# Two expert slabs of the second pair held outside the ring, loaded from GpSimd's queue

## What is computed

```python
logits = (xt @ w_router + b_router)             # 256 tokens, 32 experts
top_val, top_idx = lax.top_k(logits, 4)
gates = jax.nn.softmax(top_val, axis=-1)
...
def expert_block(args):
    xb, e = args
    hcat = xb @ w_in[e] + b_in[e]               # w_in[e]: 1024 x 2048
    x_glu = jnp.minimum(hcat[:, :D_FF], SWIGLU_LIMIT)
    x_lin = jnp.clip(hcat[:, D_FF:], -SWIGLU_LIMIT, SWIGLU_LIMIT)
    act = x_glu * jax.nn.sigmoid(SWIGLU_ALPHA * x_glu) * (x_lin + 1)
    return act @ w_out[e] + b_out[e]            # w_out[e]: 1024 x 1024
```

## Time and profile before

| | us |
|---|---|
| median of the 3 runs | 2167.94 |
| lowest and highest run | 2167.68, 2172.42 |
| profiled execution, device time | 2166.01 |
| span of its trace, first to last instruction | 2164.2 |

### The profile page before, as it was taken

How to read it: one execution, slowest core, us unless ns; L and a number is a source line. 1 busy time by engine, 2 the same in 40 slices (tenths; PEclk the granted TensorE clock), 3 DMA queues, 4 the chain that set the end, 5 groups by cost and what they waited for, 6 DMA issues and landing times.

```text
span 2164.2 us, 24146 instructions
## 1 busy us (share of the span) xinstructions
PE 2000.6 (92%) x9756; PEld 1265.9 (58%) x9756; DVE 628.3 (29%) x1299; ACT 405.4 (19%) x763; POOL 174.4 (8%) x225
## 2 busy tenths in 40 slices
PE   6999998888889898888888999999999999989998
PEld 4645643333334333333333467588788888868887
DVE  3767432111222122211122254522104316310321
ACT  3125211101111111110111120221113214320210
POOL 0000000000000000000000000000563941000000
PEclk9999999999999999999999999999999999989999
DMA  9985679999999999999999994942344342634320
GB/s 364 345 313 212 277 310 414 417 419 419 419 415 417 417 418 417 417 417 419 419 419 417 415 386 143 355 164 100 123 148 156 134 158 79 233 117 154 109 107 20
DMA packets 164389, 627.80 MB, mean 290 GB/s; under 512 B 5248, under 2 KB 9472, under 8 KB 127840
## 3 DMA queue, kind: packets, MB, share of 16 engines
q1 hardware_dynamic: 163856, 625.39, 73.8%
q0 software_dynamic: 464, 1.44, 0.2%
HBM read 625.76 MB, written 1.05 MB: 290 GB/s over the span
## 4 chain that ended last, share of the span: by engine, by line
PE 71%; DMA 16%; DVE 7%; issue 3%; ACT 2%; SPq 1%; DVEq 0%; ACTq 0%
PE psum L1007 31%; PE psum L1332 22%; DMA ring<-in_w_in_dram 14%; PE psum L1018 3%; PE psum L1309 2%; PE psum L1445 1%; PE psum L1220 1%; PE psum L1107 1%; DVE arena L2369 1%; PE psum L1620 1%; PE psum L1046 1%; DMA ring<-in_w_qkv_dram 1%; DVE arena L2384 1%; SPq L874 1%; DMA sq<-in_w_in_dram 1%
## 5 line engine op out<-in xcount | busy, mean ns | idle before, releaser
L1332 PE MATMUL psum<-ring,arena 128*64 128x512 f32 x3136 | 707.3, 608 | 90.7 <-DMA ring<-in_w_in_dram 89.9
L1007 PE MATMUL psum<-arena,ring 128*128 128x256 f32 (+1 forms) x3072 | 684.3, 385 | 6.5 <-ACT arena L1699 4.8
L1007 PEld LDWEIGHTS psum<-arena,ring 128*128 128x128 f32 x3072 | 585.3, 191 | 103.6 <-issue 22.5
L1332 PEld LDWEIGHTS psum<-ring,arena 128*64 128x64 f32 x3136 | 238.5, 140 | 546.5 <-issue 509.4
L1822 ACT ACTIVATE arena<-psum 128x512 f32<-128x512 f32 (+1 forms) x155 | 88.5, 571 | 835.8 <-PE psum L1332 726.5
L2369 DVE TENSOR_TENSOR arena<-psum,arena 128x512 f32<-128x512 f32 (+1 forms) x68 | 42.8, 668 | 431.5 <-PE psum L1354 421.7
L2356 DVE TENSOR_SCALAR arena<-consts,arena 128x64 f32<-128x64 f32 (+1 forms) x68 | 16.7, 309 | 335.0 <-PE psum L1332 335.0
L2642 DVE SCALAR_TENSOR_TENSOR consts<-psum,smalls,consts 128x255 f32<-128x255 f32 (+1 forms) x88 | 38.4, 478 | 232.7 <-ACT consts L1966 231.9
L2802 POOL DMA_DIRECT2D arena<-in_pos_dram x1 | 0.6, 577 | 1022.5 <-PE psum L1424 1022.5
L1309 PE MATMUL psum<-arena 128*128 128x256 f32 (+1 forms) x288 | 70.4, 387 | 12.0 <-DVE arena L2345 10.7
L1739 ACT ACTIVATE arena<-psum 128x512 f32<-128x512 f32 (+1 forms) x57 | 31.8, 562 | 231.6 <-PE psum L1007 175.8
(11 more groups left out here) (369 smaller groups left out, 1582.5 us busy)
## 6 DMA issues: line engine op xcount, KB each, us to landing
ring<-in_w_in_dram SPq DMA_DIRECT2D x130, 2048.0 KB, 16.2
ring<-in_w_out_dram SPq DMA_DIRECT2D x66, 2048.0 KB, 17.9
ring<-in_w_ada_dram SPq DMA_DIRECT2D x36, 2048.0 KB, 13.7
ring<-in_w_up_dram SPq DMA_DIRECT2D x22, 2048.0 KB, 8.1
ring<-in_w_ret_dram SPq DMA_DIRECT2D x12, 2048.0 KB, 15.0
ring<-in_w_down_dram SPq DMA_DIRECT2D x16, 1408.0 KB, 6.0
ring<-in_w_qkv_dram SPq DMA_DIRECT2D x4, 2048.0 KB, 19.9
ring<-in_w_rout_dram SPq DMA_DIRECT2D x4, 2048.0 KB, 9.4
```

The costliest lines, as they stand in the source:

```text
L1007: ins = nc.tensor.matmul(bank(c)[:, at:at + n], w[:, k, m * P:m * P + P], r, start=(k == 0), stop=(k == k_tiles - 1))
L1332: ins = nc.tensor.matmul(psum[at:at + CAP, p, :], act[:, k, CAP * e:CAP * e + CAP], w[:, n0:n0 + BANK], start=(k < 3 - halves), stop=(k >= ...
```

## The change

- `EARLY_SLABS` is 1: slab 2 of pair 0 still goes into the arena; slab 3 of pair 0 now goes through the ring. `slot_at` turns by one so that the slots of the later parts stay where they were.
- Two slabs of pair 1 are held outside the ring (`HELD_EXPERT = (3, 7)`, both of expert 3): slab 3 in `h_moe` and `sq` (two transfers of 1 MiB), slab 7 in `con("decay")`, `b_out_sb` and the end of `rstd` (transfers of 1 MiB, 0.5 MiB and 0.5 MiB). GpSimd issues them: slab 3 when (`htok`, 3) is ready, slab 7 when `x_ready` is 8.
- SP writes out pair 1, leaves these two out, and begins its loop at pair 2. Slab 9 of pair 1 goes into the slot that slab 3 leaves free and waits for `rows_done` 4 only. In pair 0, behind `up(0)` (`rows_done` 1) come slabs 7 and 8, behind `up(1)` slab 9, behind `up(2)` slabs 10 and 11; before, slabs 8 and 9 came behind `up(0)` and slabs 10 and 11 behind `up(2)`.
- TensorE writes out pair 1 too, with its own waits and tiles (`second_full`, `second_tile`).
- The list of extra jobs moves on DVE from behind pair 0 to behind its loop, since its buffers now hold slabs of pair 1.
- `decay` is loaded after ("rv", 0) of the retention part.

```diff
-EARLY_SLABS = 2
+EARLY_SLABS = 1
 MOE_SLABS = 12 * PAIRS - EARLY_SLABS
+HELD_EXPERT = (3, 7)
...
-    return (n + 2) % RING
+    return (n + 1) % RING
...
+        held_expert_w = [[(0, 0, flat(h_moe)), (1, 0, flat(sq))],
+                         [(0, 0, con("decay")), (1, 0, b_out_sb), (1, 1024, flat(rstd))]]
...
-                if n == 17:
-                    sp.dma_start(consts[:, at_decay:], const[:, at_decay:]).then_inc(decay_in, 16)
...
-                if q == RING:
-                    read_ready(sp, ("htok", 3))
-                    for kk, out in enumerate(early_w[1]):
-                        sp.dma_start(out, expert_source(1, 1)[:, kk, :]).then_inc(early_in[1], 16)
...
-                    sp.wait_ge(moe.rows_done, 1 if q < 8 else 3)
+                    sp.wait_ge(moe.rows_done, {6: 1, 7: 1, 8: 2, 9: 3, 10: 3}[q])
                 load(SLABS_1 + q, expert_source(j % 2, j // 2))
...
+            for j in range(12):
+                if j in HELD_EXPERT:
+                    continue
+                if j - 6 in HELD_EXPERT:
+                    sp.wait_ge(moe.rows_done, 4)
+                else:
+                    pair_left(1, j)
+                load(MOE_0 + j, expert_source(2 + j % 2, j // 2))
+            with sp.Fori(2, PAIRS) as i:
...
+                if key == ("rv", 0):
+                    sp.dma_start(consts[:, at_decay:], const[:, at_decay:]).then_inc(decay_in, 16)
...
+            experts(moe, 2, 1, second_full, second_tile)
+            with pe.Fori(2, PAIRS) as i:
...
             experts(moe, 2, 0, (0, 1), 0, (2, 3), 0, first=True)
+            with dve.Fori(1, PAIRS - 1) as i:
+                experts(moe, 2, i, (i * 2, i * 2 + 1), 0, (i * 2 + 2, i * 2 + 3), 0)
             own.mark(V.memset(sums_of[:, :, 0:64], 1.0))
...
+            for n, j in enumerate(HELD_EXPERT):
+                if n == 0:
+                    read_ready(pool, ("htok", 3))
+                else:
+                    pool.wait_ge(moe.x_ready, 8)
+                w = w_in[2 + j % 2].rearrange("(k p) n -> p k n", p=P)
+                for kk, at, out in held_expert_w[n]:
+                    pool.dma_start(out, w[:, UP_TILES * (j // 2) + kk, at:at + out.shape[1]]).then_inc(held_in[n], 16)
```

More of the change, by code:

```diff
@@ L342, in places @@
             slot[SLAB_KEYS[n]], full[SLAB_KEYS[n]] = slot_at(n), 16 * loads[slot_at(n)]
+    for j in HELD_EXPERT:
+        loads[slot_at(MOE_0 + j)] -= 1
     queue = [(slot_at(MOE_0 + n), None) for n in range(RING)]
@@ L628, in transformer_blocks_kernel @@
         over_ready = sem("over_ready")
-        early_in = [sem(f"early_in{n}") for n in range(2)]
+        early_in = sem("early_in")
+        held_in = [sem(f"held_expert_in{n}") for n in range(len(HELD_EXPERT))]
         pos_ready = sem("pos_ready")
@@ L1396, in first_full, with first_tile, loads_of, second_full @@
                     pe.wait_ge(ring_full[slot_at(n)], 16 * (n // RING + 1))
-            def first_tile(j, k_tiles, kk):
+            def first_tile(j, k_tiles, kk, n0):
                 if j == 2:
-                    return early_w[0][:, kk, :]
-                if j == 3:
-                    return early_w[1][kk]
-                return in_rows(slot_at(SLABS_1 + j if j < 2 else MOE_0 + j), k_tiles)[:, kk, :]
+                    return early_w[:, kk, n0:n0 + BANK]
+                return in_rows(slot_at(SLABS_1 + j if j < 2 else MOE_0 + j), k_tiles)[:, kk, n0:n0 + BANK]
+            def loads_of(j, held):
+                n = MOE_0 + j
+                return n // RING + 1 - sum(h % RING == j % RING for h in held)
+            def second_full(j):
+                if j in HELD_EXPERT:
+                    n = HELD_EXPERT.index(j)
+                    pe.wait_ge(held_in[n], 16 * len(held_expert_w[n]))
+                else:
+                    held = [h for h in HELD_EXPERT if h < j]
+                    pe.wait_ge(ring_full[slot_at(MOE_0 + j)], 32 + 16 * loads_of(j, held))
+            def second_tile(j, k_tiles, kk, n0):
+                if j not in HELD_EXPERT:
+                    return tile_in_ring(j, k_tiles, kk, n0)
+                for tile_k, at, w in held_expert_w[HELD_EXPERT.index(j)]:
+                    if tile_k == kk and at <= n0 < at + w.shape[1]:
+                        return w[:, n0 - at:n0 - at + BANK]
             copied(pe, ("cols", 5))
             experts(moe, 2, 0, first_full, first_tile, first=True)
-            with pe.Fori(1, PAIRS) as i:
+            experts(moe, 2, 1, second_full, second_tile)
+            with pe.Fori(2, PAIRS) as i:
                 def full(j):
-                    n = MOE_0 + j
-                    pe.wait_ge(ring_full[slot_at(n)], i * 32 + 16 * (n // RING + 1))
+                    pe.wait_ge(ring_full[slot_at(MOE_0 + j)], i * 32 + 16 * loads_of(j, HELD_EXPERT))
                 experts(moe, 2, i, full, tile_in_ring)
@@ L2438, in _ @@
             V.tensor_copy(jobs, jobs_f).then_inc(over_ready, 1)
-            with dve.Fori(1, PAIRS - 1) as i:
-                experts(moe, 2, i, (i * 2, i * 2 + 1), 0, (i * 2 + 2, i * 2 + 3), 0)
             dve.wait_ge(over_ready, 1)
```

37 lines of the change are left out of this document (18 added, 19 removed).

## The result

| | before | changed | difference |
|---|---|---|---|
| median, us | 2168.55 (2167.68 to 2172.42, 6 runs) | 2158.56 (2154.97 to 2161.78, 6 runs) | -9.99 |
| ratio to before | | 0.995 [0.9941, 0.996] | |
| profiled execution: time, span, us | 2166.01, 2164.2 | 2154.97, 2153.2 | span -11.0 |

The forecast was 2167.9 - 8.3 = 2159.6 us, with 2155.5 to 2165 as its range. It is faster by 0.5%, beyond the 0.3% that the prediction took as what a measurement can tell. The six runs of the changed kernel lie in two groups, three at 2155.0 to 2156.2 us and three at 2160.9 to 2161.8; the median stands between them.

What follows compares the result with a forecast made beforehand. Expert weight transfers at 418 GB/s were taken to bound the kernel until 1200 us. Three idle holes of 14.4 us would shrink to 6.1, gaining 8.3: 2167.9 - 8.3 = 2159.6 us, range 2155.5 to 2165.

Steps and rivals of the forecast that it cites:

- Step 1: Up to 280 us: transfers unchanged in sum, up(1)'s wait for the transfer into sq gone, TensorE 0.7 us earlier.
- Step 2: First idle hole, 280 to 284 us: slabs 7 and 8 of pair 0 still wait for up(0), so 3.3 us stay.
- Step 3: Second idle hole, 292 to 299 us: its 4.6 us vanish, as slab 9 of pair 0 waits for up(1) only.
- Step 4: Third idle hole, 318 to 326 us, 6.5 us: held slab 7 fills it, leaving holes of 0.5 and 1.9 us.
- Step 5: Turn into pair 2: TensorE no longer waits in pair 1; a 0.4 us hole remains at pair 2's slab 2.
- Step 6: Held slabs' transfers from GpSimd: the ring's rate and a start of some 4 us, hidden under work already queued.
- Steps 7 and 8: DVE's moved list (6.0 us, up to 6.0 without cover) and decay's later load (2.5 us of the engines): both cost nothing.
- Step 9: GpSimd's waits and TensorE's written-out pair 1: cost nothing, bound 1 us.
- Rival B: Held slab 7 starts too late for the third hole: gain 5.6, 2162.3 us; or clock falls in pair 1's turn, 2161.3; chance 0.27.
- C: GpSimd's queue moves the held slab slowly, up(3) of pair 1 waits, engines run dry at 365.9: slower, 2210 us; chance 0.05.
- D: The holes did not set the steady stretch's start, TensorE was late instead: nothing moves, 2167.9 us; chance 0.05.

Runs made afterwards that it cites:

- held_always: The changed kernel with slabs 3 and 7 held outside the ring in every pair from 1 to 13, issued by GpSimd: 2159.86 us, ratio 0.9949 to before.
- the extra slabs: The changed kernel with eight more unread 2 MiB slabs, one in each of pairs 4 to 11: 2196.38 us issued by GpSimd, 2198.70 us by SP.
- changed_third: The changed kernel run again with no edit, its third comparison: 2157.99 us against 2168.55 before, ratio 0.9957.
- moves_only: The kernel before with only DVE's list behind its loop and decay loaded later, no slab held: 2169.16 us against 2168.68, ratio 1.0.

## Why the prediction was right, point by point

- **What bounds** (transfers until 1200 us, everything behind shifted with them): right. In the comparisons and the traces the lack of 240 to 400 us and the time go together: 14.2 us of lack before and 14.2 with the moves alone (no gain), 2.7 and 4.2 in the changed kernel (10 to 11.5 us), 9.2 with one slab (4.7 us). "Everything behind shifted" holds for the work, but not to the microsecond: from the last `up(3)` to the end the traces differ by up to 4.8 us, mostly with the clock.
- **Step 1** (no wait for `sq`): right, the wait is gone.
- **Step 2** (the first hole of 3.3 us stays): this term was mis-sized. It measured 276 to 284 at 401 GB/s in after, at 333 and 345 in the two repeats: 0.3 to 1.6 us. The 3.3 of before held the fall of the clock at the first gather (0.72), which I took as given; with that clock in `held_always` 2.7 us stayed.
- **Step 3** (second hole gone, since slab 9 waits for `up(1)` only): right; undoing it opened 3.4 us there.
- **Step 4** (third hole closed but for 0.5 and 1.9): right for the hole, too high for what remains. Slabs 4 and 5 were issued at 325.12 in after, 327.86 and 328.08 in the repeats (predicted 329.1); in after they found the stream still busy. 326 to 330 lacks 4 x (1 - 350/418) = 0.7 us in after, 1.3 and 1.4 us in the repeats (281 and 274 GB/s).
- **Step 5** (0.4 at pair 2's slab 2): 370 to 376 moves 370 GB/s in after, a lack of 0.7 us, and 389 and 393 in the repeats, 0.4 us: right.
- **The sum**: 6.1 us of holes were to stay, 2.7 to 4.2 did, by what steps 2 and 4 had too high; small lacks that the ledger does not have (340 to 360 us at 400 to 408 GB/s) took part of it back. Where the chain of waits is read instead, the forecast is closer than its terms: pair 2's `up(3)` was to start at 409 and the last wait to end at 1192; it was 405.1, 407.9 and 408.2, and 1188.2, 1191.3 and 1191.8. With the start of before, 274.4, the changed kernel's 134.3 us would give 408.7, a gain of 8.4 us against 8.3.
- **The median** (2159.6, measured 2158.56): in part luck. The transfers gained 8.4 to 12.1 us in single traces by the clock at the first gather; the medians differ by 10.0 to 11.5. The ledger has no term for the clock there, nor for the falls of 1.7 us each behind 1200 us. Whether the change makes those rarer, or these runs happened so, stays open.
- **Step 6** (slabs from GpSimd at the ring's rate, start of 4 us): the rate is right, by the extra slabs and by landings at 276.6 and 323.1. The start of 4 us was not measured.
- **Steps 7 and 8**: right, 1.0 [0.9991, 1.0009].
- **Step 9** (written-out pair 1): nothing shows there; TensorE's only wait for a transfer in after between 300 and 380 us is 0.16 us at 339, and in `changed_third` 0.28 us.
- **Rival B** did not happen, but costs 5.3 us up to pair 2 (5.5 to 7.0 in the medians) when brought about, not 2.7. Its second part, a fall of the clock in pair 1's turn, is in none of the changed kernel's three traces: the 96 matmuls behind the turn take 20.8 us in each. **C** is out by the landings, **D** by the lack and time going together.

## What to carry to other kernels

Where transfers bound a long stretch, look for the idle holes ahead of it and treat them as one stream: a place outside the ring is worth what the later slots leave of it, and a hole closed early may only move. What is moved to a second queue must be issued before the slabs that are needed soon, for the two queues take the same engines' time: issued 9.7 us later, the second held slab was worth nothing. Before buying more buffers, compare the rate already reached with the steady one: at 417 of 418 GB/s they bought nothing that five runs could show. Where two executions are compared by their traces, first take out what TensorE's clock did in each.

## What the runs showed of the hardware

- Issued 9.7 us later, the same held slab cost 5.3 us up to pair 2's `up(3)` and 5.5 to 7.0 us in the medians, through a 3.9 us wait for a slab of the other queue and a clock of 0.79 behind that wait.
- In the steady stretch, where TensorE waits some 3 us at a time, one fall of its clock in `up(3)` (10.06 instead of 7.09 us) still left the engines 1.7 us short, so its waits there are no slack for the stream.
- The clock at the first gather was 0.72, 0.86 and 1.00 in executions with the same matmuls, and 0.86 and 1.00 in executions of one program. It moved the start of the experts by up to 3.6 us (270.88 against 274.44). The changed kernel passed that on to pair 2 (134.2 to 134.4 us behind the start in three traces); the kernels with the wait for `sq` did not (before and `moves_only`: 417.17 and 417.20 us from starts 3.0 us apart).
- Behind the last expert pair the same two pieces of TensorE's work took 10.63 or 12.3 us and 24.4 or 26 us, with the clock at 1.00 or at 0.89 and 0.94 over the stretch: 1.7 us each, in executions of programs that are the same there.
